# Eight experts in eight rounds: the rank with the half tile goes last, half-tile work is batched, and three low parts move ahead of the choices' weights

## The chip, the cores and the metric

The kernel runs on one core of a Trainium2 chip. The metric is the device time of one execution in microseconds (us), the median of several runs.

## The reference

Two transformer blocks in float32, on 256 tokens of 1024 values. The last step, the one at issue, is a mixture of experts and a normalisation:

```python
def moe_ffn(x, router_w, router_b, w1, w3, w2):
    logits = (x @ router_w).astype(jnp.float32) + router_b
    top_val, top_idx = lax.top_k(logits, TOP_K)
    weights = jax.nn.softmax(top_val, axis=-1)
    combine = jnp.sum(jax.nn.one_hot(top_idx, N_EXPERTS, dtype=jnp.float32) * weights[..., None], axis=-2)
    y = jnp.zeros_like(x)
    for e in range(N_EXPERTS):
        y = y + combine[..., e:e + 1].astype(x.dtype) * swiglu_2(x, w1[e], w3[e], w2[e])
    return y
```

Here `swiglu_2(x, w1, w3, w2)` is `(silu(x @ w1) * (x @ w3)) @ w2`, TOP_K is 2, there are 8 experts, and an expert's hidden width is 1408. The result is `layer_norm(ALPHA * x + y)`. All that comes before (attention, recurrent and dense layers) is not touched by the change.

## The kernel before, in words

**Precision.** A product that must be exact is made in three passes. A float32 weight tile is split: ScalarE copies it to float32r (the high part), VectorE subtracts that from the tile (the low part), and TensorE multiplies high x high, high x low and low x high. Where a tile of tokens is small, the kernel uses plain float32 matmuls on the unsplit weights instead.

**Ranks and tiles.** The router's choices are counted (`rank`, L2249), and the experts are ranked by the number of their tokens. Each rank has a fixed capacity: ranks 0 and 1 have two full tiles of 128 slots, rank 2 has a full tile and a half tile of 64 slots, ranks 3 to 6 have one full tile, rank 7 has one half tile. The tuple `ROUNDS` (L38) lists the rounds in order, each with its rank and tiles; before the change rank 7 stands in round 3, between rank 2 and rank 3. `TILES` numbers the tiles in that order. `HOSTED` (L40) and `GATHERS` (L47) say in which round the tokens of later tiles are gathered.

**A round.** `expert_round` exists once for each of PE (L1219), ACT (L1830) and DVE (L2380), with the same 33 steps r; all three engines work through their own list in order, held together by semaphores. A step uses one pair of weight chunks (128 x 1024 floats, 512 KB, written to one of 11 pair slots by SP, L686 to 750). Steps 0 to 21 make the hidden values in six units of two or four steps' width (`unit_pair`, L1182): unit q ends in step 3, 7, 11, 15, 19 or 21 (`UNIT_AT`, L2896). For a full tile a step is six matmuls 512 columns wide (L1059, L1062, L1063); for a half tile eight float32 matmuls 256 columns wide that write one half of the partitions each (L1193, in the last unit L1196). ACT applies silu (`hidden_silu`), DVE multiplies (`hidden_product`), PE transposes two steps later (`TURNED_AT`, L1161). Steps 22 to 32 are the down projection (`down_pair`, L1202; half tile L1212), its first half ending in step 27. ACT and DVE scale the result by the token's weight (`weighted_high` to YEH, `weighted_low` to YEL, L2377). In step 3 of the next round `back_to_tokens` (L1164) multiplies it into the output banks (L1173, half tile L1177). In step 29 `spread` (L1136; L1147, L1149) prepares the next round's tiles, and `spread_kept` (L2337) copies the result. In step 28 DVE adds a half tile's gathered tokens to one float32 copy XEB (L2402), if the next round has one.

**Splitting.** ACT and DVE split full tiles' pairs into 4 buffers, WHE (L1589) and WLE (L2291), up to three pairs ahead (`pairs_to`, `split_limit` L2990). A round with a half tile alone reads the slots directly and has no pair to split; only at its end are the first three pairs of the next round split.

**Pair slots.** SP issues the load of pair p when the slot's former pair is left: split, if only a full tile reads it, and read by the half tile's matmuls (`half_left`, L712), if there is one. SP issues in order. Ahead of round 4's first pair it issues the load of the final rows (LAST, 1024 KB, L749), which are used only in the last normalisation.

**The start of round 0.** DVE's `dispatch` (L2311) copies the low parts of the gathered tokens (L2331), computes the choices' weights (`weights`, L2295 to 2309) and copies two spreads, before its round 0 begins with the first low part of a pair. PE's `experts` (L1278) gathers, multiplies the tokens' own sums (L1133), does the two spreads, which wait for the choices' weights, and starts round 0, which waits for that low part.

**The end.** After the last round come `weighted_high`, `weighted_low` and `back_to_tokens` of the last tile's second half, then the statistics and the scaling on DVE (L2417 to 2435), and four stores.

## Time and profile before

| | us |
|---|---|
| median of three runs | 2572.97 |
| lowest and highest | 2567.89, 2573.04 |
| the profiled execution, its time | 2571.34 |
| its span | 2569.6 |
| TensorE busy, share of the span | 94% |
| round 0 begins | 2003.46 |
| round 2 (rank 2) begins | 2209.39 |
| the alone half round begins | 2308.20 |
| the round after it begins | 2351.43 |
| the last round begins | 2508.41 |

PE is TensorE's matmuls, PEld its loads of the stationary operand, DVE VectorE, ACT ScalarE, SPq the queue that issues the transfers. The end of a matmul is modelled, so consecutive matmuls overlap in the rows; their pace is read from start to start. "[idle before <-releaser]" is how long the engine stood before the row, and whose end released it. A row "x8" covers eight instructions, its time from the first start to the last end. PEclk is the granted clock of TensorE, 1.00 for 2.4 GHz and 0.50 for 1.2.

### The profile page before, as it was taken

How to read it: one execution, taken by the hardware profiler on the slowest of the kernel's cores; microseconds unless marked ns; L12 is line 12 of the kernel's file. 1: busy time of each engine (PE TensorE's matmuls, PEld its weight loads, DVE VectorE, ACT ScalarE, POOL GpSimd, SP SyncE). 2: the span in 40 equal slices, each digit the busy share in tenths (PEclk: the TensorE clock that was granted, in tenths of full speed). 3: DMA queues.
4: the chain of work that ended last, by engine and by line, in shares of the span. 5: the costliest groups of instructions: out<-in, count | busy, mean ns of one | idle time of the engine just before them, and what ended most of it. 6: DMA issues, size and time to landing. Idle time of an engine off the chain costs nothing.

```text
span 2569.6 us, 39512 instructions
## 1 busy us (share of the span) xinstructions
PE 2426.7 (94%) x14953; PEld 2012.9 (78%) x14953; DVE 1540.6 (60%) x3333; ACT 1081.7 (42%) x1972; POOL 0.2 (0%) x4
## 2 busy tenths in 40 slices
PE   7998899999888899999999899899997999999998
PEld 3853678888674899997797899887886788666886
DVE  3467553333577765647766666656857545544888
ACT  3236343223336545543303555542204444443876
POOL 0000000000000000000000000000000000000000
PEclk8999999999999999999999999999999999999999
DMA  8348423323235566543324466433322755469995
GB/s 328 91 150 279 140 83 98 102 91 99 70 95 165 171 192 184 164 144 103 91 83 143 151 191 199 147 107 94 100 74 59 250 167 165 147 177 393 340 343 213
DMA packets 182492, 410.08 MB, mean 160 GB/s; under 512 B 20256, under 2 KB 20512, under 8 KB 181792
## 3 DMA queue, kind: packets, MB, share of 16 engines
q1 hardware_dynamic: 182304, 407.56, 49.2%
q8 instruction: 120, 1.97, 0.3%
q14 instruction: 68, 0.56, 0.1%
HBM read 406.43 MB, written 1.05 MB: 159 GB/s over the span
## 4 chain that ended last, share of the span: by engine, by line
PE 88%; DVE 7%; DMA 2%; ACT 1%; issue 1%; SPq 0%; DVEq 0%; ACTq 0%
PE bank L817 11%; PE bank L821 11%; PE bank L820 11%; PE bank L1042 8%; PE bank L779 6%; PE bank L1059 6%; PE bank L1062 5%; PE bank L1063 5%; PE bank L837 3%; PE bank L840 3%; PE bank L841 3%; PE bank L969 2%; PE bank L1017 2%; PE bank L906 2%; PE bank L1193 1%; DMA ring<-stream 1%
## 5 line engine op out<-in xcount | busy, mean ns | idle before, releaser
L2206 DVE TENSOR_TENSOR WL<-ring,WH 128x512 fp32r<-128x512 f32 x632 | 411.8, 687 | 250.8 <-ACT WH L1589 249.4
L1589 ACT ACTIVATE WH<-ring 128x512 fp32r<-128x512 f32 x632 | 375.5, 625 | 299.8 <-PE bank L817 205.9
L2291 DVE TENSOR_TENSOR WLE<-slots,WHE 128x1024 fp32r<-128x1024 f32 x231 | 281.4, 1224 | 152.5 <-ACT WHE L1589 149.6
L1589 ACT ACTIVATE WHE<-slots 128x1024 fp32r<-128x1024 f32 x231 | 244.6, 1060 | 135.3 <-PE bank L1059 125.5
L817 PE MATMUL bank<-AH,WH 128*128 128x256 f32 (+1 forms) x864 | 274.0, 317 | 1.3 <-DVE WL L2206 1.3
L821 PE MATMUL bank<-AH,WL 128*128 128x256 f32 (+1 forms) x864 | 273.3, 316 | 0.0
L820 PE MATMUL bank<-AL,WH 128*128 128x256 f32 (+1 forms) x864 | 272.2, 315 | 0.0
L1042 PE MATMUL bank<-X,ring 128*128 128x256 f32 x1024 | 248.8, 390 | 5.4 <-ACT A L1589 5.4
L1042 PEld LDWEIGHTS bank<-X,ring 128*128 128x128 f32 x1024 | 190.0, 192 | 40.8 <-issue 7.6
L1059 PE MATMUL bank<-WHE,XEH 128*128 128x512 f32 (+1 forms) x432 | 166.9, 386 | 6.9 <-DVE WLE L2291 6.9
L820 PEld LDWEIGHTS bank<-AL,WH 128*128 128x128 f32 x864 | 163.4, 189 | 12.1
L821 PEld LDWEIGHTS bank<-AH,WL 128*128 128x128 f32 x864 | 162.2, 188 | 12.7
L817 PEld LDWEIGHTS bank<-AH,WH 128*128 128x128 f32 x864 | 162.3, 188 | 12.2 <-issue 1.5
L817 PE MATMUL bank<-HH,WH 128*128 128x256 f32 (+1 forms) x528 | 167.4, 317 | 0.0
L821 PE MATMUL bank<-HH,WL 128*128 128x256 f32 (+1 forms) x528 | 167.0, 316 | 0.0
L820 PE MATMUL bank<-HL,WH 128*128 128x256 f32 (+1 forms) x528 | 166.3, 315 | 0.0
L1062 PE MATMUL bank<-WHE,XEL 128*128 128x512 f32 (+1 forms) x432 | 162.4, 376 | 0.0
L1063 PE MATMUL bank<-WLE,XEH 128*128 128x512 f32 (+1 forms) x432 | 162.2, 376 | 0.0
L817 PE MATMUL bank<-PH,WH 128*128 128x256 f32 (+2 forms) x480 | 146.8, 306 | 0.0
L821 PE MATMUL bank<-PH,WL 128*128 128x256 f32 (+2 forms) x480 | 144.4, 301 | 0.0
L820 PE MATMUL bank<-PL,WH 128*128 128x256 f32 (+2 forms) x416 | 122.9, 295 | 0.0
L1589 ACT ACTIVATE A<-bank,par 128x256 f32<-128x256 f32 x60 | 28.3, 471 | 221.0 <-PE bank L1042 192.3
(345 smaller groups left out, 4776.5 us busy)
## 6 DMA issues: line engine op xcount, KB each, us to landing
ring<-stream SPq DMA_DIRECT2D x992, 256.0 KB, 2.8
slots<-experts SPq DMA_DIRECT2D x264, 512.0 KB, 5.0
con<-consts SPq DMA_DIRECT2D x1, 3204.0 KB, 12.9
X<-xin SPq DMA_DIRECT2D x1, 2048.0 KB, 9.9
par<-params SPq DMA_DIRECT2D x1, 1302.5 KB, 5.8
LAST<-final_rows SPq DMA_DIRECT2D x1, 1024.0 KB, 11.5
out<-ZO SPq DMA_DIRECT2D x4, 256.0 KB, 2.0
con<-consts SPq DMA_DIRECT2D x1, 132.0 KB, 2.7
```

The costliest lines, as they stand in the source:

```text
L779: ins = pe.matmul(o, l, r, start=start, stop=stop)
L817: ins = pe.matmul(o, wh, hi(kk), start=kk == 0, stop=False)
L820: read_signal(pe.matmul(o, wh, lo(kk), start=False, stop=False))
L821: ins = pe.matmul(o, wl, hi(kk), start=False, stop=kk == k - 1)
L837: ins = pe.matmul(o, wh, hi(kk, tt), start=kk == 0, stop=False)
L1042: ins = pe.matmul(o, weight(st["n"]), X[:, kk, 0:T], start=kk == 0, stop=kk == KD - 1)
L1059: ins = pe.matmul(o, hi, WHE[:, s, at:at + w], start=start, stop=False)
L1062: pe.matmul(o, lo, WHE[:, s, at:at + w], start=False, stop=False)
L1063: return pe.matmul(o, hi, WLE[:, s, at:at + w], start=False, stop=stop)
L1589: return nc.scalar.activation(o, i, fn, **kw)
L2206: V.tensor_tensor(WL[:, s % SPLIT, :], ring[:, c % RING, :], WH[:, s % SPLIT, :].bitcast(F32), ALU.subtract).then_inc(w_taken, 1)
L2291: V.tensor_tensor(WLE[:, s % PAIR_SPLIT, :], pair(pair_of(s)), WHE[:, s % PAIR_SPLIT, :].bitcast(F32), ALU.subtract).then_inc(pair_taken, 1)
```

## The change

It has three parts. (1) In `ROUNDS` rank 7 with its half tile moves from round 3 to round 7, the last. What depends on the order follows: the slots of CE for half tiles, the wait for XEB, the last half tile's closing matmuls, and `split_limit` of a round without a full tile. The load of the final rows is issued ahead of round 1's first pair. (2) In rank 2's round PE no longer does the half tile's step behind each step of the full tile. `HALF_STEPS` lists after which steps the half tile catches up: four steps at a time in the units, two in the last unit, three or two in the down projection. (3) DVE splits three pairs before it computes the choices' weights, and the two first spreads and their copies stand at step 2 of round 0.

```diff
--- before.py
+++ after.py
@@ -35,7 +35,7 @@
 HID = 2 * FH * P
 EXPERTS = 8
 FULL, HALF = "full", "half"
-ROUNDS = ((0, (FULL, FULL)), (1, (FULL, FULL)), (2, (FULL, HALF)), (7, (HALF,)), (3, (FULL,)), (4, (FULL,)), (5, (FULL,)), (6, (FULL,)))
+ROUNDS = ((0, (FULL, FULL)), (1, (FULL, FULL)), (2, (FULL, HALF)), (3, (FULL,)), (4, (FULL,)), (5, (FULL,)), (6, (FULL,)), (7, (HALF,)))
 TILES = [(k, rank, 1 if kind is HALF else n, kind) for k, (rank, kinds) in enumerate(ROUNDS) for n, kind in enumerate(kinds)]
 HOSTED = {0: 1, 1: 2, 2: 3, 4: 4, 6: 5}
 H = P // 2
@@ -745,7 +745,7 @@
                                             skip_runtime_bounds_check_because="an index of one of the eight experts")
                              for j in range(EXPERTS)]
                 k, r = divmod(p, TILE_PAIRS)
-                if k == 4 and r == 0:
+                if k == 1 and r == 0:
                     sp.dma_start(LAST[:, :, :], final_rows).then_inc(last_in, 16)
                 sp.dma_start(pair(p), experts[bass.ds(which[ROUNDS[k][0]] * TILE_PAIRS + r, 1)]).then_inc(pair_loaded[p % PAIR_SLOTS], 16)
 
@@ -1174,8 +1174,9 @@
                                                     start=False, stop=last and y is YEL)
                                 else:
                                     for g in range(2):
-                                        pe.matmul(o[:, g * T:(g + 1) * T], CE[:, half_slot(i, g), t * P:(t + 1) * P],
-                                                  y[:, i % 2, half * T:(half + 1) * T], start=False, stop=False)
+                                        ins = pe.matmul(o[:, g * T:(g + 1) * T], CE[:, half_slot(i, g), t * P:(t + 1) * P],
+                                                        y[:, i % 2, half * T:(half + 1) * T], start=False,
+                                                        stop=last and y is YEL and g == 1)
                             if last:
                                 ins.then_inc(e_sum, 1)
 
@@ -1216,6 +1217,15 @@
                 if kind is HALF and blocks[-1] < 2 * FH - 1:
                     ins.then_inc(pair_read, 1)
 
+            def pair_step(k, r, i, side, kind):
+
+                p, q = TILE_PAIRS * k + r, min(r // 4, UNITS - 1)
+                if r < 22:
+                    per = 2 if q < UNITS - 1 else 4
+                    unit_pair(k, p, q, range((r - 4 * q) * per, (r - 4 * q + 1) * per), i, side, kind)
+                else:
+                    down_pair(k, p, (2 * r - 44, 2 * r - 43), i, side, kind)
+
             def expert_round(k):
 
                 hosted = HOSTED.get(k)
@@ -1231,7 +1241,7 @@
                             pe.wait_ge(e_kept, first_tile(k + 1))
                             pe.wait_ge(e_yl, 2 * first_tile(k - 1) + tiles_of(k - 1))
                         if HALF in ROUNDS[k][1]:
-                            pe.wait_ge(e_xb, k - 1)
+                            pe.wait_ge(e_xb, sum(HALF in kinds for _, kinds in ROUNDS[:k + 1]))
                     elif r == 4:
 
                         if k == 0:
@@ -1258,11 +1268,15 @@
                     else:
                         pe.wait_ge(pair_loaded[p % PAIR_SLOTS], 16 * (p // PAIR_SLOTS + 1))
                     for i, side, kind in sides(k):
-                        if r < 22:
-                            per = 2 if q < UNITS - 1 else 4
-                            unit_pair(k, p, q, range((r - 4 * q) * per, (r - 4 * q + 1) * per), i, side, kind)
+                        if kind is FULL or alone(k):
+                            pair_step(k, r, i, side, kind)
                         else:
-                            down_pair(k, p, (2 * r - 44, 2 * r - 43), i, side, kind)
+
+                            for n in HALF_STEPS.get(r, ()):
+                                pair_step(k, n, i, side, kind)
+                    if k == 0 and r == 2:
+                        spread(0)
+                        spread(1)
                     if r == 3 and k:
                         back_to_tokens(k - 1)
                     if r in TURNED_AT:
@@ -1281,8 +1295,6 @@
                 for n in range(8):
                     gather(0, n)
                 own_sums()
-                spread(0)
-                spread(1)
                 for k in range(len(ROUNDS)):
                     expert_round(k)
                 back_to_tokens(len(ROUNDS) - 1)
@@ -2330,9 +2342,6 @@
                     dve.wait_ge(e_gathered, n + 1)
                     V.tensor_copy(XEL[:, 2 * n - 8:2 * n - 6, :, :].rearrange("p a b c -> p (a b c)"),
                                   gathered_bank(0, n)[:, :]).then_inc(e_xl, 1)
-                weights()
-                spread_kept(0)
-                spread_kept(1)
 
             def spread_kept(i):
 
@@ -2381,7 +2390,14 @@
 
                 following = sides(k + 1) if k + 1 < len(ROUNDS) else []
                 for r in range(TILE_PAIRS):
+                    if k == 0 and r == 0:
+
+                        pairs_to(3)
+                        weights()
                     pairs_to(split_limit(k, r + 1 + PAIRS_AHEAD))
+                    if k == 0 and r == 2:
+                        spread_kept(0)
+                        spread_kept(1)
                     if r in UNIT_AT:
                         hidden_product(k, UNIT_AT[r])
                     if r in TURNED_AT:
@@ -2893,6 +2909,8 @@
     return sum(min(c + 1, hi) - lo + (c >= hi) for lo, hi in WHOLE if lo <= c)
 
 
+HALF_STEPS = {3: range(0, 4), 7: range(4, 8), 11: range(8, 12), 15: range(12, 16), 19: range(16, 20), 21: (20, 21),
+              24: (22, 23, 24), 27: (25, 26, 27), 30: (28, 29, 30), 32: (31, 32)}
 UNIT_AT = {3: 0, 7: 1, 11: 2, 15: 3, 19: 4, 21: 5}
 TURNED_AT = {5: 0, 9: 1, 13: 2, 17: 3, 21: 4}
 
@@ -2992,8 +3010,7 @@
     rounds = split_rounds()
     if k not in rounds:
 
-        upto = TILE_PAIRS * sum(n < k for n in rounds)
-        return upto + PAIRS_AHEAD if ahead == TILE_PAIRS + PAIRS_AHEAD else upto
+        return TILE_PAIRS * sum(n < k for n in rounds)
     at = TILE_PAIRS * rounds.index(k)
     stretch = TILE_PAIRS if k + 1 not in rounds else ahead
     return at + min(ahead, stretch)
@@ -3001,7 +3018,7 @@
 
 def half_slot(i, g):
 
-    return i % 4 if g == 0 else i - 1
+    return i % 4 if g == 0 else 4 + i // 8
 
 
 def gathered_units(g):
```

## Rows read from the trace of the kernel before

**Rows 1.** The page, busy time of each engine
```profile
PE 2426.7 (94%) x14953; PEld 2012.9 (78%) x14953; DVE 1540.6 (60%) x3333; ACT 1081.7 (42%) x1972; POOL 0.2 (0%) x4
```
**Rows 2.** The page, costliest groups: the two parts of a pair
```profile
L2291 DVE TENSOR_TENSOR WLE<-slots,WHE 128x1024 fp32r<-128x1024 f32 x231 | 281.4, 1224 | 152.5 <-ACT WHE L1589 149.6
L1589 ACT ACTIVATE WHE<-slots 128x1024 fp32r<-128x1024 f32 x231 | 244.6, 1060 | 135.3 <-PE bank L1059 125.5
```
**Rows 3.** Windows: us, each engine's busy us (instructions), granted clock, transfers' share, GB/s
```profile
2003.40:2008.00 4.60, 4.54 (x13) 3.64 (x14) 3.33 (x3) 0.00 (x0) 0.00 (x0) 0.63 1.03 408
2209.40:2299.00 89.60, 87.83 (x492) 56.86 (x492) 46.83 (x66) 43.41 (x59) 0.00 (x0) 1.00 0.57 165
2308.20:2346.30 38.10, 38.04 (x302) 24.77 (x298) 5.50 (x17) 2.61 (x8) 0.00 (x0) 1.00 0.96 363
2351.40:2356.40 5.00, 4.97 (x13) 3.99 (x14) 4.37 (x5) 3.42 (x4) 0.00 (x0) 0.55 1.03 408
2440.00:2508.00 68.00, 68.00 (x340) 57.10 (x339) 59.71 (x68) 53.68 (x66) 0.00 (x0) 1.00 0.95 340
```
**Rows 4.** Timeline around the start of round 0: start us, us, engine, line
```profile
1997.00 1.29 DVE L2331 CAST XEL<-bank 128x512 fp32r<-128x512 f32 x2 [0.23 <-PE bank L1125]
...
1998.69 1.06 ACT L1589 ACTIVATE WHE<-slots 128x1024 fp32r<-128x1024 f32 x1 [0.22 <-DMA slots<-experts]
...
1999.02 0.39 PE L1133 MATMUL bank<-XTL,SAME 128*128 128x512 f32 x1
...
2000.04 0.17 DVE L2306 TENSOR_TENSOR S<-S 128x8 f32<-128x8 f32 x1
...
2000.26 0.44 PE L1147 MATMUL bank<-con,PICK 128*128 128x128 f32 x2 [0.86 <-DVE S L2306]
...
2001.16 0.50 PE L1149 MATMUL bank<-S,PICK 128*128 128x1 f32 x4
...
2003.46 0.47 PE L1059 MATMUL bank<-WHE,XEH 128*128 128x512 f32 x1 [1.80 <-DVE WLE L2291]
```
**Rows 5.** Timeline of TensorE, two half-tile steps of the third round
```profile
2213.46 1.08 PE L1193 MATMUL bank<-slots,XEB 128*64 128x256 f32 x8
...
2216.06 1.08 PE L1193 MATMUL bank<-slots,XEB 128*64 128x256 f32 x8
```
**Rows 6.** Timeline of TensorE, the alone half round and the round after it
```profile
2337.18 5.40 PE L1212 MATMUL bank<-slots,HB 128*64 128x256 f32 x48
2342.51 0.44 PE L1147 MATMUL bank<-con,PICK 128*128 128x128 f32 x2
...
2366.23 0.39 PE L1062 MATMUL bank<-WHE,XEL 128*128 128x512 f32 x1
...
2367.59 0.39 PE L1062 MATMUL bank<-WHE,XEL 128*128 128x512 f32 x1
...
2369.18 0.39 PE L1063 MATMUL bank<-WLE,XEH 128*128 128x512 f32 x1
...
2369.86 0.39 PE L1062 MATMUL bank<-WHE,XEL 128*128 128x512 f32 x1
```
**Rows 7.** Timeline between the alone half round and the next
```profile
2345.22 0.63 PEld L1212 LDWEIGHTS bank<-slots,HB 128*64 128x64 f32 x8 [0.51 <-DMA slots<-experts]
2348.97 1.06 ACT L1589 ACTIVATE WHE<-slots 128x1024 fp32r<-128x1024 f32 x1 [7.97 <-DMA slots<-experts]
...
2351.43 0.77 PE L1059 MATMUL bank<-WHE,XEH 128*128 128x512 f32 x1 [5.13 <-DVE WLE L2291]
```
**Rows 8.** Timeline of the end; groups by form, 256 columns wide, 2308.2 to 2351.4
```profile
2556.98 0.69 ACT L1589 ACTIVATE YEH<-bank,WEIGHT 128x512 fp32r<-128x512 f32 x1 [4.15 <-PE bank L1063]
...
2557.70 0.75 DVE L2377 SCALAR_TENSOR_TENSOR YEL<-bank,WEIGHT,YEH 128x512 fp32r<-128x512 f32 x1 [3.41 <-ACT YEH L1589]
...
L2377 DVE SCALAR_TENSOR_TENSOR YEL<-bank,WEIGHT,YEH 128x256 fp32r<-128x256 f32 x2 | 1.0, 483 | 3.6 <-ACT YEH L1589 3.5
L1589 ACT ACTIVATE YEH<-bank,WEIGHT 128x256 fp32r<-128x256 f32 x2 | 0.9, 474 | 5.5 <-PE bank L1212 5.5
```

## What the change will do to the time

> **What bounds the kernel now.** I read the page first. TensorE is busy for 94% of the span [rows 1], so time is saved only where TensorE waits, where its clock is down, or where its instructions run closer together. Per pair of expert weights the other engines need 1.06 us (ScalarE, high part) and 1.22 us (VectorE, low part) [rows 2]. Then the windows by stage [rows 3]. In the third round (128-slot and 64-slot tile together) TensorE is busy 87.8 of 89.6 us at full clock, and the transfers use 0.57 of their engines. In the last rounds of one full tile TensorE is busy all the time, VectorE 59.7 of 68 us, transfers 0.95. So neither is limited by transfers, though the later one has little to spare. Two further windows in these rows have a mean granted clock of 0.63 and 0.55: in part of each TensorE runs at 1.2 instead of 2.4 GHz, right after a stretch in which it waited.
>
> **Part A, the low parts before the choices' weights.** Before, VectorE finishes the last low part of the gathered tokens at 1998.29 and then computes the choices' weights; TensorE ends its sums (last start 1999.02), does two spreads from 2000.26 to 2001.66, and begins round 0 at 2003.46, behind the first low part of a weight pair [rows 4]. Three high parts lie ready by then (the fourth ends at 1999.75). After: VectorE starts the first low part at 1998.3, 1.22 us [rows 2] and about 0.1 for the signal, so TensorE starts at 1999.6, 3.9 us earlier. The spreads' 1.4 us are not saved; they go behind the third pair. Net 2.5 us. VectorE is then done with three low parts at 2002.0 and, with some 2.0 us of small instructions (the last of them starts at 2000.04 [rows 4]), with the choices' weights at 2004; the fourth low part follows at 2005.3. A step of two full tiles is 12 matmuls of 0.227 us [rows 6], 2.7 us, so the spread is asked for near 2007.7 and pair 3 after that: both are covered by about 3 us. If that cover were gone, the spread would wait for the weights, at most the 2.0 us. The kept copies have another step of 2.7 us before TensorE asks for them. The SP queue is not touched here.
>
> The slow stretch behind the gap: a mean of 0.63 over 4.6 us [rows 3] is 1.7 us lost; single steps give 1.6. With no wait longer than 0.3 us from 1997 on, I expect it to vanish: 1.6 us. The other end is 0, if it is owed to the thin work well before. The only sign is that it starts behind the gap, as does the one in part C, so I take 1.6. **A = 4.1.**
>
> **Part B, the 64-slot tile a unit behind.** Before, each of the 33 steps of this round is six 512-wide matmuls of the full tile and eight 256-wide ones of the half tile; from the start of one such eight to the next is 2.60 us [rows 5]. On their own the six take 1.36 us (start to start of six in a row), and 48 half-tile matmuls in a row take 5.33 us, 0.89 per eight [rows 6]. So 0.35 us per step is lost in changing over, once to the half tile and once back. The change keeps every matmul and leaves 10 changes for 33: 23 x 0.35 = 8.05. Against that, six transposes or spreads that now stand behind a half tile will stand between full-tile matmuls; there, one matmul, two transposes and another matmul take 0.68 us where the parts give about 0.58 (two at 0.227, two at 0.065 by my estimate) [rows 6], so 6 x 0.1 = 0.6 back. **B = 7.5.** Bounds: 0, if the loss belongs to each eight and not to the change; 8.1, with no price for the transposes.
>
> What could stall here: after a batch of four half steps (3.6 us) ScalarE reads the half tile's unit first and then makes the next high part. From the batch's end that is about 0.5 for the signal and the read (my estimate, by its 128 columns), 1.06 and 1.22 [rows 2] and 0.2 for a signal, about 3.0 us, and TensorE has three split pairs in hand, 4.1 us. The transposes of the unit are asked for after two steps, 2.7 us, and the product is there after about 1. So I cost it at nothing; without that cover each batch would pay the difference. SP waits in order for the half tile's reads, and four pairs of eleven are held up to 9 us; at 0.57 busy the transfers make that up. The waits before the down weights and before their second half stay, since the same instructions follow the same last matmul.
>
> **Part C, rank 8 last.** Before, the alone half round takes 38.1 us for 33 pairs [rows 3]. One pair of 524288 bytes at 408 GB/s [rows 3] takes 1.28 us, and 33 take 42.4, so the round uses up what was loaded ahead, and a 1 MB load of the final rows (2.6 us at that rate) goes into the same stretch. The next round's first pair comes late: ScalarE waits 7.97 us for it, TensorE 5.13 [rows 7]. After: behind rank 3's round stands a full round whose pairs are in and whose first three are split; this wait goes, 5.1 us. So does the slow clock after it: 0.55 over 5.0 us is 2.2 us. The half round's own short wait for a load, 0.51 us [rows 7], goes too, because it now follows a full round, whose slots are freed at the split, three steps ahead, and the 1 MB load is issued in round 1 between others at about half load. What I charge: the sum into XEB (1024 columns on VectorE, as many as a low part, so 1.22 us [rows 2]; before beside 2.6 us steps) now falls in a round of 1.36 us steps, while the kept copies, the weighted low part and two low parts are due. VectorE would be done with the last low part about when it is asked for: 0.3. **C = 5.1 + 2.2 + 0.5 - 0.3 = 7.5.** Bounds: 10 us if more loads' waits go than I see, 2.5 if the loads are late in the last round (rival 2).
>
> The Trainium skill ("DMA: Bandwidth & Descriptors", Anatomy of one DMA) gives about 2.0 us plus bytes over 436 GB/s, an estimate of 3.2 us for such a pair. If the 22 loads that wait for a slot of the last round were served one after the other at that price, the round would take 70 us instead of 37; by that the change would lose. No row bears it out: 408 GB/s [rows 3] is only reached with the fixed part overlapped.
>
> **Part D, the end.** The last chain is YEH, YEL, second half to tokens: 0.69 and 0.75 us for 512 columns, 0.474 and 0.483 for 256 [rows 8]. The final VectorE work hangs on it. **D = 0.5.** The matmuls back to tokens keep their number of columns.
>
> **The sum.** 4.1 + 7.5 + 7.5 + 0.5 = 19.6 us. The profiled execution has a time of 2571.34 (span 2569.6, 1.7 around it): 2551.7. The median of the runs is 1.6 above the profiled one and one run 3.5 below it, so I say 2552. A measurement of this kernel can tell about 0.2%, 5 us, from no change.
>
> **Rivals.**
> 1. *The loss sits in each half step, not in the change-over.* B is then near 0: 2571.3 - 12.1 = 2559. For it: in this round the trace shows step and change only together. Against: 48 in a row run at 0.111 us each with the same loads [rows 6]. 12%.
> 2. *The last round is bound by its loads.* 42.4 us of transfers against about 37 of TensorE (38.1 less the wait and the spread): +5, that is 2557. For: transfers at 0.95 in the rounds before. Against: eleven pairs are ahead at its start, and before it met the same need with 0.5 us of waiting. 9%.
> 3. *The slow clock stays at both places* (or falls elsewhere): 3.8 less, 2555.5. [...] 8%.
> 4. *Slower: the batches starve the full tile.* Place: the step after each of the ten batches. ScalarE stands in its queue at the half tile's unit, and no high part is made meanwhile. If three split pairs don't last, TensorE waits, up to the batch's 3.6 us each time; ten make 36 us, 2571.3 - 19.6 + 36 = 2588. It decides against the change from 2.0 us per batch on. Against: the chain of 3.0 us against 4.1. 3%.
> 5. *No change to speak of*: B lost, and half of C and A given back. 3%.
>
> **The numbers.** The forecast itself has 65%, with a range of its own from 2547 to 2556 (run to run 2.5 us each way, B by 1, A and C by 1.5). To take in rivals 1 to 3 the range goes up to 2560, and down to 2547. Faster by over 0.2% in the forecast and rivals 1 to 3: 0.94; same 0.03; slower 0.03.
>
> **What the changed profile would show.** A: the first round-0 matmul 0.4 us behind the last of the own sums; full clock there. B: half-tile matmuls in groups of 32 (24 in the down part), spaced 0.111 us, and ten changes, in a round shorter by 7.5 us. C: no wait of more than 1 us between rounds, the last 37 us in fp32 matmuls with ScalarE and VectorE nearly idle, no wait for slots there. D: YEH and YEL of 256 columns in the last chain. I would be wrong if WLE is named as a releaser of TensorE after the batches, or if the groups of 32 still cost 0.35 us per eight.

## The result and the profile after

The changed kernel took 2557.98 us (median of 7 runs, 2545.59 to 2560.74) beside 2572.97 for the kernel before: a ratio of 0.9935 [0.9918, 0.9951], 16.7 us less. Measured once more, it took 2551.52 (6 runs, 2543.08 to 2560.09) beside 2570.82: 0.9924 [0.9899, 0.9948], 19.5 us less. The forecast was 2552, with 2547 to 2560, and a gain of 19.6 us.

The profiled execution after has a time of 2545.59 and a span of 2543.8, 25.8 us less than the one before. That is more than either ratio says; most of this section is about which part of the 25.8 belongs to the change. The page of the profile, busy time and the two groups of weight splits (share of the span, count; busy, mean ns, idle before):

```profile
PE 2410.0 (95%) x14953; PEld 2006.5 (79%) x14953; DVE 1541.0 (61%) x3333; ACT 1082.2 (43%) x1972; POOL 0.2 (0%) x4
...
L2303 DVE TENSOR_TENSOR WLE<-slots,WHE 128x1024 fp32r<-128x1024 f32 x231 | 281.3, 1224 | 130.0 <-ACT WHE L1601 126.5
L1601 ACT ACTIVATE WHE<-slots 128x1024 fp32r<-128x1024 f32 x231 | 244.6, 1061 | 111.7 <-PE bank L1059 110.7
```

The splits cost what they did [rows 2]; TensorE's share went up [rows 1]. Timeline of the kernel after at the four places that the change touches: start of round 0, first batch of half-tile steps, end of the third round, start of the last (start us, us, engine, line):

```profile
1991.79 3.49 DVE L2303 TENSOR_TENSOR WLE<-slots,WHE 128x1024 fp32r<-128x1024 f32 x3
...
1992.57 0.39 PE L1133 MATMUL bank<-XTL,SAME 128*128 128x512 f32 x1
...
1993.15 0.47 PE L1059 MATMUL bank<-WHE,XEH 128*128 128x512 f32 x1 [0.19 <-DVE WLE L2303]
...
2217.36 0.39 PE L1063 MATMUL bank<-WLE,XEH 128*128 128x512 f32 x1
2217.68 3.67 PE L1194 MATMUL bank<-slots,XEB 128*64 128x256 f32 x32
2221.29 0.50 PE L1059 MATMUL bank<-WHE,XEH 128*128 128x512 f32 x1
2221.62 0.40 PE L1062 MATMUL bank<-WHE,XEL 128*128 128x512 f32 x1
...
2227.34 3.67 PE L1194 MATMUL bank<-slots,XEB 128*64 128x256 f32 x32
...
2288.48 1.95 PE L1213 MATMUL bank<-slots,HB 128*64 128x256 f32 x16
...
2290.36 0.50 PE L1059 MATMUL bank<-WHE,XEH 128*128 128x512 f32 x1
...
2495.84 0.39 PE L1063 MATMUL bank<-WLE,HEH 128*128 128x512 f32 x1
...
2531.54 0.50 PE L1177 MATMUL bank<-YEH,CE 128*128 128x256 f32 x2
...
2532.23 0.48 DVE L2386 SCALAR_TENSOR_TENSOR YEL<-bank,WEIGHT,YEH 128x256 fp32r<-128x256 f32 x1 [4.57 <-ACT YEH L1601]
```

Round 0 now begins 0.58 us behind the last own sum; before it was 4.44 [rows 4]. 32 half-tile matmuls stand in a row, 0.113 us each, with one change-over in front (2217.36 to 2217.68, 0.32 where 0.227 is usual) and one behind (2221.29 to 2221.62, 0.33). The last YEL is 256 wide and takes 0.48 instead of 0.75 [rows 8].

The kernel after by stretches (us, busy time and count of PE, PEld, DVE, ACT and POOL, granted clock, DMA share, GB/s): start of round 0, the third round, the four rounds of one full tile, the last round, the end:

```profile
1993.10:1998.00 4.90, 4.85 (x21) 4.05 (x22) 4.69 (x12) 1.06 (x1) 0.00 (x0) 1.00 1.03 420
2198.70:2290.40 91.70, 89.81 (x547) 66.10 (x546) 51.10 (x69) 47.33 (x63) 0.00 (x0) 1.00 0.52 178
2290.40:2496.10 205.70, 205.70 (x1022) 172.68 (x1020) 179.55 (x204) 160.64 (x197) 0.00 (x0) 1.00 0.94 340
2496.10:2531.30 35.20, 35.12 (x279) 22.19 (x278) 4.56 (x14) 2.83 (x8) 0.00 (x0) 1.00 0.90 343
2531.30:2543.80 12.50, 2.63 (x20) 1.98 (x16) 8.89 (x16) 2.55 (x5) 0.00 (x0) 0.75 0.23 84
```

Where the clock was 0.63 and 0.55 [rows 3] it is 1.00. What TensorE's matmuls still wait for from 2000 to 2543, and for transfers its weight loads (PEld) from 2480 on (total us, times, longest):

```profile
PE bank L1059 <- issue: 2.2, 3, 0.7
PE bank L1059 <- DVE HEL L2365: 2.1, 2, 1.0
PE bank L1059 <- DVE HB L2370: 1.0, 1, 1.0
...
PEld bank L1213 <- DMA slots<-experts: 0.7, 2, 0.5
```

No WLE is among them: neither the batches nor the start of the last four full rounds starve TensorE of split weights. The last line stands at the very end of the last round and is taken up with `last_late`.

**The account.** Both executions are divided at the same instructions: the start of the last own sum, of round 0, of the third round, of the next round, of the last half unit's way to tokens, and the span's end. Worked out from the trace, us:

```
                          before    after   change   forecast
own sum to round 0          4.44     0.58    -3.86   } A -4.1
rounds 0 and 1            205.93   205.60    -0.33   }
third round                98.81    91.61    -7.20   B -7.5
five rounds behind it     248.52   241.18    -7.34   C -7.5
end                        12.88    12.26    -0.62   D -0.5
sum                       570.58   551.23   -19.35   -19.6
```

The other 6.45 us of the 25.8 lie before 1999, in work that the change does not touch. That part goes with the execution and is taken up behind the experiments.

### The profile page after: what moved, and what is told of

The parts are those of the page before. It is cut to its first block, busy times and chain, and to the rows that moved or that the text cites. A ratio compares the mean times of both kernels' runs of the same rounds, so it can differ in the third digit from the quotient of the medians.

```text
span 2543.8 us, 39512 instructions
## 1 busy us (share of the span) xinstructions
PE 2410.0 (95%) x14953; PEld 2006.5 (79%) x14953; DVE 1541.0 (61%) x3333; ACT 1082.2 (43%) x1972; POOL 0.2 (0%) x4
## 3 DMA queue, kind: packets, MB, share of 16 engines
HBM read 406.43 MB, written 1.05 MB: 160 GB/s over the span
## 4 chain that ended last, share of the span: by engine, by line
PE 87%; DVE 8%; DMA 2%; issue 1%; ACT 1%; SPq 0%; DVEq 0%; ACTq 0%
PE bank L817 11%; PE bank L820 11%; PE bank L821 11%; PE bank L1042 8%; PE bank L1059 6%; PE bank L779 6%; PE bank L1063 5%; PE bank L1062 5%; PE bank L837 3%; PE bank L840 3%; PE bank L841 3%; PE bank L969 2%; PE bank L1017 2%; PE bank L906 2%; PE bank L1194 1%; DMA ring<-stream 1%
```

## Experiments

In the texts on record, T1 is the working of the prediction, every part worth its own term; another name (T2 or a rival) stands for what is set beside it there. Diffs are against the kernel before for the single parts and for the load alone, else against the changed kernel. I read each by stage, since stages that neither the edit nor a slow clock touches repeat within some 0.1 us from execution to execution (the last round within 0.7), while whole times do not. Each run has one profile, so a row of the table is one execution. The stages, us: from the last own sum to round 0; then to the first step-3 call of back_to_tokens, from each call to the next, and the end (worked out from the traces):

```
             own>r0  >1     1>2    2>3   3>4   4>5   5>6   6>7   7>8   end   sum
before        4.5  112.85 103.38 92.07 47.33 53.01 49.06 52.68 42.88 12.88 570.6
after         0.6  112.51 102.23 88.04 50.83 53.00 49.06 50.94 31.78 12.26 551.2
again         0.6  112.52 102.24 88.04 50.83 53.00 49.06 50.94 31.48 12.32 551.0
a_only        0.6  112.50 103.38 92.07 45.75 53.01 49.07 52.68 42.87 12.79 564.7
b_only        4.5  113.92 102.20 85.93 47.46 53.01 49.07 52.68 42.87 12.81 564.4
c_only        4.4  113.90 103.37 94.22 50.84 52.99 49.07 50.93 31.77 12.29 563.8
b_two         0.6  112.50 102.58 89.46 50.84 52.99 49.07 50.93 31.71 12.25 552.9
b_six         0.6  112.55 102.21 87.30 50.83 53.00 49.06 50.94 31.62 12.29 550.4
last_late     0.5  112.48 102.22 88.06 50.83 52.99 49.07 50.94 33.00 12.29 552.4
no_low        2.5  112.50 102.23 88.05 50.84 52.99 49.07 50.93 32.15 12.25 553.5
l_only        4.4  112.88 103.41 92.08 43.46 53.01 49.07 52.67 42.88 12.80 566.7
last_k4       0.6  112.52 102.22 88.06 50.84 52.99 49.07 50.93 31.96 12.31 551.5
turn_early    0.6  111.21 100.92 86.77 51.27 53.43 49.56 51.52 31.97 12.33 549.6
turn_six      0.6  111.22 100.91 86.05 51.32 53.48 49.46 51.45 31.67 12.32 548.5
```

### The whole again, and each part alone

`again` is the changed kernel unaltered. `a_only` makes part A alone: the spreads move behind the third pair, the three low parts ahead of the choices' weights. `b_only` makes part B alone, `c_only` the order of rounds, with the place of the load of the final rows and the 256-wide end (parts C and D). The main lines of their edits, abridged:

```diff
a_only
+                    if k == 0 and r == 2:
+                        spread(0)
+                        spread(1)
...
+                    if k == 0 and r == 0:
+
+                        pairs_to(3)
+                        weights()
b_only
-                        if r < 22:
...
+                        if kind is FULL or alone(k):
+                            pair_step(k, r, i, side, kind)
                         else:
...
+                            for n in HALF_STEPS.get(r, ()):
+                                pair_step(k, n, i, side, kind)
c_only
-ROUNDS = (... (2, (FULL, HALF)), (7, (HALF,)), (3, (FULL,)), ...)
+ROUNDS = (... (2, (FULL, HALF)), (3, (FULL,)), ..., (7, (HALF,)))
...
-                if k == 4 and r == 0:
+                if k == 1 and r == 0:
```

> The changed kernel once more. T1 (the three parts add up, and the spread between executions lies in stretches that the change does not touch): round 0 begins 0.6 us behind the last of the own sums, round 2 takes 91.6 us, from the start of round 3 to the last down matmul 241 us, the tail 12.5 us; the start of round 0 may lie several us off the 1993.15 of the first profile. T2 (TensorE runs at one of two paces while it is granted full clock, drawn when the clock rises; the change removes two such rises, so one draw holds for 550 us): executions spread over some 15 us again (2545 to 2561), and in a slow one the 512-wide matmuls of the rounds start 0.235 us apart where they start 0.227 us apart in the first profile.

> Part A alone: three low parts ahead of the choices' weights, spreads at step 2 of round 0; order of rounds and half-tile steps as before. T1: 4.1 us less than before, of which 1.6 us is the slow clock that no longer follows the start of round 0; waits of 5.1 us and the slow clock behind the half round stay. T2: the same mean, but the rounds from 1994 to 2351 run on one draw of the pace, so executions spread more than before and less than with all parts.

> Part B alone: half-tile steps of rank 2's round in ten batches. T1 (the loss is in the change-over): round 2 shorter by 7.3 us, the time by 7.3 us. Rival (the loss is in each eight): round 2 as long as before, 98.8 us. T2: spread as before, since both rises of the clock stay.

> Part C alone: rank 7 last, final rows loaded in round 1; start of round 0 and half-tile steps as before. T1: 7.5 us less, plus 0.4 at the end; no wait over 1 us between rounds. Rival (loads bind the last round): the last round over 37 us, up to 42. T2: one draw of the pace holds from 2008 to the end, so executions spread more than before.

Measured, beside 2570.82 (29 runs, 2561.94 to 2584.32): again 2551.52, ratio 0.9924 [0.9899, 0.9948]; a_only 2568.07 (12 runs), 0.9979 [0.9962, 0.9997]; b_only 2568.21 (12), 0.9991 [0.9971, 1.001]; c_only 2565.25 (12), 0.9981 [0.9964, 0.9998]. In us the three parts are 5.4, 2.3 and 4.9 by the ratios, each with some 4 to 5 us of uncertainty: too coarse to size a part. The stages do it: 5.9, 6.2 and 6.8, together 18.9 of the 19.35. Two lengths of slow clock explain nearly all that the single figures are off their terms. In b_only and c_only the stretch behind the gap at round 0 is slower than in the profile of before, though their edits do nothing there: 113.9 instead of 112.85, 1.05 us. Window of b_only behind that gap:

```profile
2006.50:2011.10 4.60, 4.55 (x11) 3.62 (x12) 3.31 (x3) 0.00 (x0) 0.00 (x0) 0.50 1.03 410
```

0.50 over 4.6 us where before had 0.63 [rows 3]; l_only below has 0.63 too. What differs is the granted clock some 20 us earlier, in the same work, the normalisation and the router ahead of the choices. Windows of c_only and of l_only at the same distance ahead of the last own sum:

```profile
1970.00:1990.00 20.00, 14.99 (x54) 8.64 (x54) 10.40 (x34) 8.10 (x21) 0.00 (x0) 0.74 0.00 0
...
1963.00:1983.00 20.00, 13.90 (x84) 9.98 (x83) 12.17 (x40) 8.44 (x21) 0.00 (x0) 1.00 0.00 0
```

b_only has 0.74 there as c_only has, and before 1.00 as l_only has. So the longer slow stretch goes with how the execution ran ahead of the gap; with two profiles on each side, that it is the cause is not shown. And in a_only the round behind the alone half round is 1.6 us shorter (45.75 for 47.33): it waited 4.32 us there and not 5.13, and the clock behind it was 0.66 over 5 us and not 0.55. Part A's own stretch in a_only:

```profile
1999.80:2004.80 5.00, 4.92 (x22) 4.11 (x23) 4.79 (x12) 1.06 (x1) 0.00 (x0) 1.00 1.03 417
```

Gap of 0.58, clock 1.00: A takes the gap and the slow clock both. (117.35 to 113.1 for gap and first stage, 4.2 us.) B alone, stages "1>2" and "2>3": 1.2 + 6.1 = 7.3. C with D alone, against before: 2.15 lost in "2>3" (where the alone half round's cheap first steps stood), 3.51 more in "3>4", 1.75, 11.11 and 0.6 less behind: 7.8 us. 4.2, 7.3 and 7.8 are 19.3 of the 19.35: the parts are independent, they add up.

### What the change-over costs: batches of two and of six

```diff
b_two
-HALF_STEPS = {3: range(0, 4), ..., 30: (28, 29, 30), 32: (31, 32)}
+HALF_STEPS = {**{r: (r - 1, r) for r in (1, 3, 5, ..., 31)}, 32: (32,)}
b_six
+HALF_STEPS = {**{4 * q + 3: range(4 * q, 4 * q + 4) for q in range(5)},
+              21: (20, 21), 27: range(22, 28), 32: range(28, 33)}
```

> The changed kernel with the half tile catching up after every second step: 17 batches instead of 10. Read from the stage between two calls of back_to_tokens (step 3 of round 2 to step 3 of round 3, 88.04 us in the changed kernel, and round 1 to round 2, 102.2). T1 (a fixed price per change-over, 0.32 us by 7.3 us for 23): the two stages together 2.2 us longer. Rival (the gain needs whole units, or comes from elsewhere than the change-over): the same as with ten, or as long as before (195.45 together).

> The changed kernel with two batches in the down projection (six and five steps) instead of four: 8 batches. T1: 0.6 us shorter. Rival (the batches begin to starve the full tile, or the six held slots stop the loads): longer, with WLE named as releaser of TensorE in round 2 or 3, by up to the 2.7 us that a batch grows.

Times, one run each beside 2573.64: 2551.29 and 2547.24. The stages "1>2" and "2>3" together: b_two +1.77 for 17 batches instead of 10, b_six -0.76 for 8. For b_six that is 0.38 us for each of two changes saved; the prediction had 0.35. The rows give the same. 16 half-tile matmuls take 1.88 us (2218.94 to 2220.82 below) and 32 take 3.61 (2217.68 to 2221.29 above), 0.108 each and 0.15 for every row of them. So eight in a row cost 0.86, and 2.60 - 1.36 - 0.86 is 0.38.

For b_two T1 had 2.2; seven changes at 0.38 are 2.7, so 0.9 is missing. Timeline of TensorE in b_two, a batch with the transposes behind it, and the batch one unit (four steps) later:

```profile
2218.62 0.39 PE L1063 MATMUL bank<-WLE,XEH 128*128 128x512 f32 x1
2218.94 1.95 PE L1194 MATMUL bank<-slots,XEB 128*64 128x256 f32 x16
2220.82 0.55 PE L1161 MATMUL bank<-con,HE 128*128 128x128 f32 x3
2221.12 0.48 PE L1059 MATMUL bank<-WHE,XEH 128*128 128x512 f32 x1
...
2228.88 1.95 PE L1194 MATMUL bank<-slots,XEB 128*64 128x256 f32 x16
```

From one batch to the batch a unit later, the same 24 full-tile and 32 half-tile matmuls and three transposes take 9.94 us here and 9.66 in the changed kernel (2217.68 to 2227.34). One change more costs 0.28 and not 0.38, because the transposes stand behind a half tile again: they are dearer by 0.1 between full-tile matmuls, as T1 had it. Four sets of transposes and one of spreads are 0.5 of the 0.9. Most of the rest stands in front of the first gather of the down projection. Timeline of TensorE in the changed kernel:

```profile
2259.81 0.48 PE L1059 MATMUL bank<-WHE,HEH 128*128 128x512 f32 x1
...
2261.57 1.18 PE L1125 MATMUL bank<-PICK,XTH 128*128 128x256 f32 x8
...
2267.87 0.40 PE L1059 MATMUL bank<-WHE,HEH 128*128 128x512 f32 x1
...
2269.26 1.12 PE L1125 MATMUL bank<-PICK,XTL 128*128 128x256 f32 x8
```

Six full-tile matmuls and then the gather: 1.76 us the first time, 1.39 later. In b_two, as in the kernel before, half-tile work stands in that place. The 0.37 is what batching gives back there; VectorE's copy HB ends just ahead of the gather, at 2261.42, but no run tries whether that is what it waits for.

One of the 23 changes that T1 counted saved nothing. In the last unit the half tile is multiplied as 128 columns, not twice 64 (L1196 before, L1197 after). From the first full-tile matmul of its two steps to the transposes behind them, in the kernel before with two half-tile steps apart, and in the changed kernel with them together:

```profile
2266.19 0.39 PE L1059 MATMUL bank<-WHE,XEH 128*128 128x256 f32 x1
...
2272.60 0.49 PE L1161 MATMUL bank<-con,HE 128*128 128x128 f32 x3
...
2250.25 0.39 PE L1059 MATMUL bank<-WHE,XEH 128*128 128x256 f32 x1
...
2256.67 0.49 PE L1161 MATMUL bank<-con,HE 128*128 128x128 f32 x3
```

6.41 us and 6.42. So the price belongs to the changes between the 128-column and the 64-column form; where both kinds have 128 columns there is none. (The full tile's matmuls are 256 wide there and not 512; that was not tried apart.) With all of it, 22 x 0.38 - 6 x 0.1 - 0.4 = 7.4, where part B measured 7.2 to 7.3. Rival 1, a loss in each half step, would have left both stages where they were; it falls.

### The last round and its loads

```diff
last_late
-                if k == 1 and r == 0:
+                if k == 7 and r == 12:
                     sp.dma_start(LAST[:, :, :], final_rows).then_inc(last_in, 16)
```

> The changed kernel with the 1 MB load of the final rows ahead of pair 12 of the last round, in the midst of the loads that wait for slots. T1 (the last round is bound by TensorE; 22 loads of 1.28 us behind its first read end near 30 us of its 35): the last round at most 0.5 us longer. Rival (loads bind the last round): the whole 2.6 us show, as a wait for slots in the down projection.

One run: 2549.65. The stage "7>8" is 33.00, where the nine other profiles with this last round have 31.48 to 32.15 (31.78 and 31.48 in the two of the changed kernel). That is 0.9 to 1.5 us of the 2.6 that the 1 MB load takes of the queue. T1 had at most 0.5, so it missed. TensorE's waits for slots in last_late, in the wait view of its weight loads (PEld) and matmuls (total us, times, longest):

```profile
PEld bank L1213 <- DMA slots<-experts: 2.5, 4, 0.7
...
PE bank L1213 <- DMA slots<-experts: 0.5, 3, 0.2
```

The last three of these places in its timeline:

```profile
2532.08 1.08 PE L1213 MATMUL bank<-slots,HB 128*64 128x256 f32 x8 [0.20 <-DMA slots<-experts]
2533.35 1.08 PE L1213 MATMUL bank<-slots,HB 128*64 128x256 f32 x8 [0.19 <-DMA slots<-experts]
2534.59 0.65 PE L1213 MATMUL bank<-slots,HB 128*64 128x256 f32 x4 [0.15 <-DMA slots<-experts]
```

The pairs of the last steps now arrive one by one, 1.27 us apart, and each is waited for. But the changed kernel itself has no slack there. Its last pair lands at 2530.49 (worked out from the trace), and the weight loads that read it wait:

```profile
2530.53 0.63 PEld L1213 LDWEIGHTS bank<-slots,HB 128*64 128x64 f32 x8 [0.54 <-DMA slots<-experts]
```

In nine of the ten profiles with this last round, last_late among them, the stage ends 1.06 us behind the landing of the last pair, and in `again`, the shortest, 1.16 us behind it. So the last load sets the end of the round, and how late it lands is the 0.7 us by which the stage varies. In last_late it lands 1.2 us later than in the changed kernel's first profile, counted from the same call; about 1.4 of the 2.6 found the queue idle. So rival 2, a last round bound by its loads, did come true in nine of ten, at a cost of up to 0.7 us and not 5. That the stage's length follows the landing is read from the traces; no run gave the round more slack.

### The low parts, taken out again

```diff
no_low
                     if k == 0 and r == 0:
 
-                        pairs_to(3)
                         weights()
```

> The changed kernel without the three low parts ahead of the choices' weights; the spreads stay at step 2. T1: round 0 begins 2.0 us later (2.6 instead of 0.6 behind the last of the own sums), and all else stays: total from the own sums 553.2 instead of 551.2. Rival (the gap brings the slow clock back): 1.6 us more, 554.8.

One run: 2552.80. Timeline of TensorE at the start of round 0 in no_low:

```profile
1997.50 0.39 PE L1133 MATMUL bank<-XTL,SAME 128*128 128x512 f32 x1
1999.99 0.47 PE L1059 MATMUL bank<-WHE,XEH 128*128 128x512 f32 x1 [2.10 <-DVE WLE L2303]
```

The window behind it (columns as in the windows above):

```profile
2000.00:2004.00 4.00, 4.00 (x18) 3.33 (x19) 3.25 (x3) 0.71 (x1) 0.00 (x0) 1.00 1.02 412
```

The gap is 2.49 instead of 0.58: +1.9, as expected of the 2.0 us of small instructions. But the clock stays at 1.00, so the rival falls. A has two halves: moving the spreads alone, which is what no_low has against before, gives 2.3 us by gap and first stage (117.3 to 115.0: 1.95 less gap and the slow clock gone, against 1.4 of spreads paid later), and the low parts ahead of the weights give the other 1.9.

### The load of the final rows, in the old and in the new order

```diff
l_only (against before)          last_k4 (against the changed kernel)
-   if k == 4 and r == 0:        -   if k == 1 and r == 0:
+   if k == 1 and r == 0:        +   if k == 4 and r == 0:
```

> The kernel before with nothing changed but the load of the final rows, ahead of round 1's first pair instead of round 4's. T1 (the wait behind the half round is a debt of 42.4 us of pairs and 2.6 us of final rows against 38 us of TensorE): the 5.1 us wait of TensorE shrinks by 2.6 us, to 2.5; what the slow clock does after it is open (0 to 2.2 us). Rival (the order of the rounds is not needed, the load alone did it): the wait goes. Rival (the load is beside the point): 5.1 us as before.

> The changed kernel with the load of the final rows back ahead of round 4's first pair, now in the full rounds. T1: the same as the changed kernel within 0.3 us (stages 50.83, 53.0, 49.06, 50.94), since these rounds leave the transfers 5% free and eleven pairs ahead. Rival (full rounds are near enough to their loads): up to 2.6 us in the stage of round 3 or 4.

One run each beside 2574.89 (11 runs): 2565.22 and 2552.24. l_only against before: "3>4" falls from 47.33 to 43.46, 3.9 us, and nothing else moves. Timeline of l_only behind the alone half round:

```profile
2345.79 0.47 PE L1059 MATMUL bank<-WHE,XEH 128*128 128x512 f32 x1 [2.01 <-DVE WLE L2291]
```

Its window from there on:

```profile
2346.00:2350.00 4.00, 4.00 (x12) 3.14 (x12) 3.94 (x5) 3.33 (x4) 0.00 (x0) 0.63 1.03 410
```

The wait of 5.13 [rows 7] is 2.01, 3.1 us less where T1 had 2.6, and the slow clock behind it is 0.8 us shorter: one line of the change, made alone, gives half of part C. In last_k4 the same line undone costs 0.3 us of 551.5, one WLE wait of 0.2: with rank 7 last (the prediction, counting from 1, calls it rank 8), the place of this load is worth nothing that can be told from the last round's own 0.7. The gain is the same hole filled from two sides; it must not be counted twice. (C's 7.34 against l_only's 3.9: the order is still worth 3.4 on top.)

### Would transposes a step earlier do better?

The two waits for HEL and the one for HB, 1.0 us each, are what is left in the wait view of the changed kernel.

```diff
turn_early
-TURNED_AT = {5: 0, 9: 1, 13: 2, 17: 3, 21: 4}
+TURNED_AT = {5: 0, 9: 1, 13: 2, 17: 3, 20: 4}
```

`turn_six` is turn_early with b_six's batches.

> The changed kernel with unit 4's transposes one step earlier (step 20 instead of 21), on all three engines. T1 (the 1.0 us wait ahead of the down projection in rounds 0 to 2 is the low part of unit 4, asked for right behind its transposes): the three waits of 1.0 us go, 3 us less, total from the own sums 548.2; in rounds of one tile the transposes may wait up to 0.3 us each for the product. Rival (the wait moves to the transposes, since the product is not ready a step earlier): no gain, or slower in the rounds of one tile.

> The changed kernel with both: eight batches and unit 4's transposes at step 20. T1: 3 + 0.7 us less than the changed kernel, 23 less than before, a ratio of 0.991. Rival: the transposes wait as said, and it is the changed kernel's time.

turn_early, one run, 2540.04; turn_six 2549.15 (6 runs, 2544.03 to 2558.86), ratio 0.9912 [0.989, 0.9934]. TensorE's waits in turn_early from 2000 on:

```profile
PE bank L1059 <- issue: 2.2, 3, 0.7
PE bank L1161 <- DVE HE L2378: 1.0, 4, 0.2
```

The waits of 1.0 are gone (1.3 us less in each of the first three rounds), and four of 0.25 came in the rounds of one full tile, where a step is half as long and the unit is not ready a step earlier: +0.45 in each of those. Net -1.6 by stages for turn_early, -2.7 for turn_six, where T1 had -3 and -3.7: the first three rounds gave 3.9 together, and the 2.0 that the four rounds of one tile lose stood in no total of T1's. Two cautions. The 2540.04 is not 12 us better than the changed kernel: its touched part is 549.6 against 551.2, the rest is the draw described below. And 0.9912 and 0.9924, the ratios of turn_six and of the changed kernel, cannot be told apart. Earlier transposes in the rounds with two tiles alone would by the stages give about 546.7 (548.5 less 4 x 0.45); that was not tried.

## The other 6.45 us

The last own sum starts at 1999.02 before and 1992.57 after, in code that is the same. Over the 14 profiles this mark lies anywhere from 1988.7 to 2004.0, and what lies behind it repeats as said above. So nearly all of the spread between the profiled executions lies ahead of the mark; for the runs without a profile (22 us in 29 runs of before, 17 in six of again) that is inferred. Two windows of TensorE in the kernel before, both at full granted clock (us, PE busy and count, granted clock, DMA share, GB/s):

```profile
940.00:960.00 20.00, 20.00 (x173) 1.00 0.67 198
...
1500.00:1520.00 20.00, 20.00 (x179) 1.00 0.68 192
```

The same in the changed kernel's first profile:

```profile
940.00:960.00 20.00, 20.00 (x179) 1.00 0.69 202
...
1500.00:1520.00 20.00, 20.00 (x179) 1.00 0.66 194
```

And in `again`, the same program once more:

```profile
1500.00:1520.00 20.00, 20.00 (x173) 1.00 0.64 194
```

173 matmuls in 20 us or 179, with the same busy share, clock and nearly the same transfers. The timeline at these places shows 256-wide matmuls that start either 117.7 or 113.3 ns apart, for 100 us and more; they keep one pace between places where the granted clock falls and rises, and may leave such a place with the other. From 890 to 1050 three of 14 profiles ran at the slower pace (before, a_only, c_only), at 1500 to 1600 six (again, b_only, no_low, l_only, last_k4, turn_six). About 1470 matmuls at 4.4 ns more are 6.5 us for one such stretch, about what this pair of profiles differs by. The 512-wide matmuls of the rounds start 227 ns apart in every profile, so the rounds don't take part, and T2 falls in that: it had expected 235 ns there in a slow execution. Its spreads did not come either (19.5 us in a_only, 30.6 in b_only, 13.9 in c_only, 22.4 before). Nine of the 14 profiles, before among them, have one such slow stretch, and no edit touches these places; I put neither gain nor loss down to it. What chooses the pace stays open; none of the runs was made to turn it.

The pace is not the whole spread. The five profiles without a long slow stretch (after, b_two, b_six, last_late, turn_early) still have the mark from 1988.7 to 1996.6. A second part is the granted clock ahead of the choices, shown for c_only above: b_two has 0.74 there too, and over the last 50 us ahead of the mark b_only, c_only and b_two take 5.4 us longer than turn_early, b_six, last_late and last_k4 2.6, and the rest the same within 0.1 (worked out from the traces). What starts this stretch is as open.

## Why the prediction was right, and where it was not

- **The whole.** Forecast 19.6 us, 19.35 by stages, 16.7 and 19.5 by the two ratios. The medians of 2557.98 and 2551.52, 6.5 us apart for one program, are both in the range. The step that was badly sized is "run to run 2.5 us each way": three runs of before (2567.9 to 2573.0) were too few to show a spread of 22 us. The first median lies outside the forecast's own range (to 2556) while the stages hold to 0.25 us of the sum. Part of that closeness is luck: in B and C errors of 0.3 to 0.8 us cancel.
- **A, 4.1: 4.2.** Gap of 0.58, which is the working's own 1999.6 less 1999.02 (the 0.4 in its list of signs does not fit it); both spreads hidden, slow clock gone. That the slow clock goes with the long gap is shown by a_only (gap 0.58, clock 1.00) and no_low (wait 2.10, clock 1.00) against before and l_only (4.4, 0.63), b_only and c_only (4.4, 0.50); the spreads stood in the gap each time, so length and content are not told apart. Rival 3 is out. The thin work before round 0 alone did not bring it down, and with a 2.1 us wait in no_low it did not either, yet a wait of 2.01 us in l_only, behind a dense half round, was followed by 0.63 over 4 us. So the length of one wait does not decide it. The Trainium skill ("TensorE: Matmul & The Clock Gate", Part 1) says that the clock is set by how busy TensorE has been recently. These rows agree only so far that a wait of 2.0 to 2.1 us was followed by either level; of the two, it was the one behind the denser stretch that had the slow clock after it, so they do not show that rule by themselves.
- **B, 7.5: 7.2.** The mechanism is right. The price of a change, 0.35, is 0.38: the 0.89 for eight half-tile matmuls was a sixth of a row of 48, the start of that row included, and eight inside a row cost 0.86. The 0.1 for transposes and spreads held. Two things were overlooked and nearly cancel the first: the change inside the last unit costs nothing (22 changes count, not 23), and the first gather of the down projection starts 0.4 us late without a half-tile step in front of it. No WLE wait behind any batch, so rival 4 had no ground, and rival 1 is refuted by b_two and b_six.
- **C, 7.5: 7.3.** The wait of 5.1 and the slow clock behind it went. Two small terms did not hold. "The half round's own short wait for a load, 0.51, goes too": it stays in most executions (0.7 us in the profile after, the longest 0.54 at 2530.53; 1.0 in last_k4; none in again), since the last loads of the round come 1.28 us apart and a step of eight half-tile matmuls takes 0.9. The cause given, slots freed three steps ahead, is right for the round's start only. And the 0.3 charged for the sum into XEB was not paid: no wait shows at 2496. The last round took 35.2 us, not "37"; it now carries back one full tile's results instead of one and a half, and that work went to another round. Left out of the working was that one line of the change, the load, gives half of C in the old order, and nothing in the new.
- **D, 0.5: 0.6.** YEH and YEL of 256 columns in the last chain, 0.47 and 0.48.
- **Rival 2**, the last round bound by its loads, had the place and the cause right, and the size wrong. The working set 42.4 us of transfers against 37 and took eleven pairs ahead as ample. They are just enough: the last pair lands as it is asked for. The last round moved 343 GB/s over 35.2 us, and last_late's pairs came 1.27 us apart, as 524288 bytes at 408 to 420 GB/s do. The estimate of 3.2 us for a pair after the Trainium skill ("DMA: Bandwidth & Descriptors", Anatomy of one DMA) would give 3.2 us from each landing to the next only if the transfers came one after the other; that section is on transfers issued from GpSimd, and these are issued by SyncE. At 1.27 us apart the trace shows the fixed part overlapped, as the prediction said.

## What to carry to other kernels

Where small and large matmuls alternate, price the change between them from two rows (the alternating step, and each kind in a row of its own), then batch up to what the split weights in hand cover: here 0.38 us a change, and 7 us of a 19 us gain. Look at the form of each: where the small ones used all 128 columns, the change was free. A light-compute, load-bound step belongs where loads can run ahead of it and nothing follows it. Then compare when its last load lands with when it is read: here they met. Before reordering, look at whether a big load that nobody needs yet sits in that step's queue, since moving it alone may give half the gain. Size a change of under 1% by stages between like instructions in two traces, not by two medians: most stages repeated within 0.1 us where whole runs of the same program differed by 17 to 22.

## What the runs showed that I had not expected

- At a granted clock of 1.00, stretches of 256-wide matmuls have two paces, 113.3 and 117.7 ns, kept from one dip of the clock to another and worth some 6.5 us for one such stretch; 512-wide ones have one, 227 ns.
- Changing between full-array matmuls 512 wide and half-tile ones on 64 columns cost 0.38 us there and back; between full-array ones 256 wide and half-tile ones on 128 columns, nothing (6.41 and 6.42 us).
- After the same gap of 4.4 us the clock was 0.63 over 4.6 us in two profiles and 0.50 in two others, 1.05 us apart in the stage, with the same work behind it. The two with 0.50 had also run at a mean of 0.74 over 20 us ahead of the choices, the other two at 1.00.
- A 1 MB load nobody waits for cost the kernel before 3.1 us of wait and 0.8 of clock, by standing among the loads of a round that had no slack.
